# A two-layer trunk on one core: four modulation units of the second layer moved from the first layer's attention to the second's

## The reference

```python
def _modulation(cond, w, b):                       # w: 1024 x 6144, per layer
    m = jax.nn.silu(cond) @ w + b
    return tuple(t[:, None, :] for t in jnp.split(m, 6, axis=-1))

for l in range(2):
    sh, sc, g, shf, scf, gf = _modulation(cond, w_mod[l], b_mod[l])     # once for each group
    h = _adaln(x, norm_mix[l], sh, sc)             # rmsnorm(x) * (1 + sc) + sh
    x = x + g * (attention(h @ w_in[l]) @ w_out[l])    # l = 0: GQA and differential, l = 1: windowed
    n = _adaln(x, norm_ffn[l], shf, scf)
    scores = softmax(n @ w_router)                 # 16 experts, best group of 4, top 2 in it
    x = x + gf * sum_e gate_e * ((silu(n @ w_gate[l, e]) * (n @ w_up[l, e])) @ w_down[l, e])
```

## Time and profile before

| | |
|---|---|
| three runs | 1251.59, 1253.26, 1253.58 us; median 1253.26 |
| the profiled execution | 1251.47 us, of which 1249.7 us from the first to the last instruction |
| PE matmuls | busy 1170.3 us, 94% |
| DVE, ACT, POOL | 280.0, 187.2 and 56.4 us |
| DMA | 494.13 MB, mean 395 GB/s; the SP's queue fills 93.9% of 16 engines' time |
| chain that ended last | PE 73%, DMA 20%, issue 4% |
| first layer | attention to 195 us, experts to 634 us |
| second layer | attention to 806 us, experts to 1243 us, outputs to the end |

### The profile page before, as it was taken

One profiled execution on the slowest core, in us unless ns is written; L12 is line 12 of the kernel. 1 busy time (PEld: TensorE's weight loads), 2 busy tenths in 40 slices (PEclk: granted clock), 3 DMA queues, 4 the chain that ended last, 5 costly groups with the idle time before them and its releaser, 6 DMA issues.

```text
span 1249.7 us, 13688 instructions
## 1 busy us (share of the span) xinstructions
PE 1170.3 (94%) x5491; PEld 511.9 (41%) x5491; DVE 280.0 (22%) x677; ACT 187.2 (15%) x439; POOL 56.4 (5%) x68
## 2 busy tenths in 40 slices
PE   4999999999988998998999999999999899889998
PEld 2445454443423343333344454653434334343433
DVE  1146533121010102020233253312021110102013
ACT  1224322010000000000122342210001101000010
POOL 0412000000000000000013020000000000000000
PEclk9999999999999999999999999999999999999999
DMA  9999999999999999999994578899999999999997
GB/s 375 388 365 382 417 417 430 422 431 427 425 427 428 428 428 428 428 429 428 419 386 150 214 287 329 333 405 425 422 387 428 428 427 428 428 430 428 428 423 306
DMA packets 62820, 494.13 MB, mean 395 GB/s; under 512 B 5795, under 2 KB 6963, under 8 KB 31285
## 3 DMA queue, kind: packets, MB, share of 16 engines
q1 hardware_dynamic: 59728, 485.85, 93.9%
q0 software_dynamic: 2864, 7.46, 1.9%
q10 hardware_dynamic: 180, 0.17, 0.0%
HBM read 490.69 MB, written 3.16 MB: 395 GB/s over the span
## 4 chain that ended last, share of the span: by engine, by line
PE 73%; DMA 20%; issue 4%; ACT 1%; DVE 1%; SPq 1%; POOL 0%; DVEq 0%; POOLq 0%
PE bank L1131 40%; PE bank L902 12%; DMA ring<-in_w_gate 10%; DMA ring<-in_w_up 7%; PE bank L912 3%; PE bank L1090 3%; PE bank L1099 3%; PE bank L858 3%; PE bank L1157 2%; DMA ring<-in_w_in_ab 2%; PE bank L834 2%; DMA ring<-in_w_down 1%; PE bank L1187 1%; PE bank L950 1%; PE bank L1170 1%
## 5 line engine op out<-in xcount | busy, mean ns | idle before, releaser
L1131 PE MATMUL bank<-ring,hT 128*64 128x512 f32 x2592 | 595.0, 609 | 53.2 <-issue 23.4
L1131 PEld LDWEIGHTS bank<-ring,hT 128*64 128x64 f32 x2592 | 199.0, 140 | 417.2 <-issue 415.7
L902 PE MATMUL bank<-ring,hT 128*128 128x512 f32 x320 | 141.9, 601 | 3.1 <-DMA ring<-in_w_in_ab 2.4
L902 PEld LDWEIGHTS bank<-ring,hT 128*128 128x128 f32 x320 | 60.4, 192 | 80.0 <-issue 77.4
L1905 DVE TENSOR_TENSOR work<-work,bank 128x512 f32<-128x512 f32 x56 | 38.5, 688 | 188.8 <-PE bank L1099 188.6
L1898 DVE TENSOR_TENSOR work<-work,bank 128x512 f32<-128x512 f32 x32 | 22.0, 687 | 229.6 <-PE bank L1131 198.6
L1090 PE MATMUL bank<-work 128*128 128x128 f32 x512 | 61.5, 279 | 0.0
L1090 PEld LDWEIGHTS bank<-work 128*128 128x128 f32 x512 | 59.9, 195 | 1.7 <-issue 1.6
L1448 ACT ACTIVATE hT<-bank 128x512 f32<-128x512 f32 x32 | 19.0, 595 | 255.7 <-PE bank L1187 255.7
L912 PE MATMUL bank<-ring,work 128*128 128x512 f32 x128 | 56.5, 594 | 0.3 <-DVE work L1722 0.3
L1946 DVE COPY work<-bank 128x512 f32<-128x512 f32 x14 | 9.7, 692 | 206.3 <-PE bank L1131 206.3
(11 more groups left out here) (214 smaller groups left out, 729.6 us busy)
## 6 DMA issues: line engine op xcount, KB each, us to landing
ring<-in_w_gate SPq DMA_DIRECT2D x58, 2048.0 KB, 17.1
ring<-in_w_up SPq DMA_DIRECT2D x50, 2048.0 KB, 17.2
ring<-in_w_down SPq DMA_DIRECT2D x50, 2048.0 KB, 16.9
ring<-in_w_mod SPq DMA_DIRECT2D x23, 2048.0 KB, 11.3
work<-in_w_up SPq DMA_DIRECT2D x8, 2048.0 KB, 15.5
ring<-in_w_down SPq DMA_DIRECT2D x16, 1024.0 KB, 13.7
ring<-in_w_in_c SPq DMA_DIRECT2D x6, 2048.0 KB, 20.6
ring<-in_w_in_ab SPq DMA_DIRECT2D x4, 2048.0 KB, 21.6
```

The lines of the kernel that those rows point to most:

```text
L902: ins = pe.matmul(b[:, 0:n], hT[:, c, t * P:(t + 1) * P], w[:, c, 0:n], start=i == 0, stop=i == DC - 1)
L1131: ins = pe.matmul(bank[banks[j]][64 * e:64 * e + 64, :], lhs[:, 4 * h + c, 64 * e:64 * e + 64], weights(e, c, j), start=(h, c) == (0, 0), ...
```

## The change

Four things change together.

1. The four units `("mod", 1, 1, k)` leave the first layer's list and the end of `dense_units(0)`. They are loaded behind the input projection of the second layer, and PE uses them at the points "scores" (two), 0 and 1 of the second layer's attention. The group's transposes stand at point 2, and group 2 follows one turn later, with two of its units at point 3.
2. The first expert units of the first layer go straight into the freed slots (`free` is 4 in place of 0; 3 in place of 2 in the second layer), and both layers load the first waiting units in halves.
3. The shift's logits of the second layer are computed in its routing, as in the first layer; and the token rows' logits there stand ahead of the second output projection. Their place in `last_scatter` is taken by `keep_busy(8)`.
4. The first projection of a layer waits for all modulated rows again; `keep_busy(7)` stands ahead of it in the second layer, and `keep_busy` of 8 takes the place of the two units that stood in the first layer's routing.

The diff, cut to its core:

```diff
-        (6,): [("mod", 1, 1, 0)],
         6: [("oT", 0)],
-        (7,): [("mod", 1, 1, 1)],
-        7: [("hT", 1, 1), ("wo", 0, 0), ("rt", 1), ("hk", 1), ("wo", 1, 0), ("rc",), ("xT",), ("mod", 1, 1, 2),
-            ("rt", 0), ("hT", 1, 0), ("mod", 1, 1, 3), ("hk", 0), ("pos",), ("nextT", 1)]},
+        7: [("hT", 1, 1), ("wo", 0, 0), ("rt", 1), ("wo", 1, 0), ("rc",), ("xT",),
+            ("rt", 0), ("hT", 1, 0), ("hk", 0), ("pos",)]},
...
-        "scores": [("in", 2, 0), ("in", 3, 0)],
-        0: [("in", 4, 0)],
-        1: [("T", 0), ("mod", 1, 2, 0), ("in", 5, 0)],
-        2: [("mod", 1, 2, 1)],
-        3: [("mod", 1, 2, 2)],
+        "scores": [("in", 2, 0), ("mod", 1, 1, 0), ("in", 3, 0), ("mod", 1, 1, 1)],
+        0: [("in", 4, 0), ("mod", 1, 1, 2)],
+        1: [("T", 0), ("mod", 1, 1, 3), ("in", 5, 0)],
+        2: [("modT", 1), ("mod", 1, 2, 0)],
+        3: [("mod", 1, 2, 1), ("mod", 1, 2, 2)],
...
-        7: [("hT", 1, 1), ("wo", 0, 0), ("hk", 1), ("wo", 1, 0), ("rt", 1), ("xT",),
+        7: [("hT", 1, 1), ("wo", 0, 0), ("rt", 1), ("wo", 1, 0), ("rc",), ("xT",),
             ("rt", 0), ("hT", 1, 0), ("hk", 0), ("pos",)]}}
...
     if kind == "rt":
-        return [("rt", l, rest[0])]
+        return [("rt", l, rest[0])] + (banks_of(l, ("hk", 1)) if rest[0] else [])
...
-        return mods(0, 0) + inputs + mods(0, 1) + mods(0, 2) + mods(1, 0) + out + mods(1, 1)
+        return mods(0, 0) + inputs + mods(0, 1) + mods(0, 2) + mods(1, 0) + out
     scales = mods(1, 2)
-    return inputs + scales[0:2] + out + scales[2:4]
+    return inputs + mods(1, 1) + scales[0:2] + out + scales[2:4]
...
-                free = 2 * l
+                free = (4, 3)[l]
...
-                if l == 1:
-                    load_halves(0, MOE_UNITS - 2, 1)
-                    load_halves(1, 0, 2)
-                else:
-                    for k in range(SLOTS + AHEAD, MOE_UNITS):
-                        load_early(0, k)
+                load_halves(0, MOE_UNITS - 2, 1)
+                load_halves(1, 0, 2)
...
-                first = (u, t) == (0, 1)
                 for h in range(2):
-                    if not first:
-                        pe.wait_ge(*emptied_by(("hT", l, 0, t, h)))
-                for i in range(DC):
-                    c = 4 * ((i + 1) % 2) + i // 2
-                    if first and i < 6:
-                        pe.wait_ge(chunk_ready[("dve", "act")[i % 2]], 3 * l + i // 2 + 1)
+                    pe.wait_ge(*emptied_by(("hT", l, 0, t, h)))
...
-                if l == 1:
-                    pe.wait_ge(mod_emptied, 6)
-                    keep_busy(2)
+                pe.wait_ge(mod_emptied, 4 + 2 * l)
+                keep_busy(2 if l else 8)
...
                         if (l, t) == (0, 1):
-                            shift_logits(1)
+                            keep_busy(8)
...
-                keep_busy(3 if l else 2)
+                keep_busy(3)
...
                 if l == 1:
                     norm(1, 0, 1)
+                    keep_busy(7)
```

More of the change, by code:

```diff
@@ L434, in build @@
         one, other = ("modT", 0, 0), ("hT", 0, 0, 1, 1)
-        done_at[one], done_at[other] = done_at[other], done_at[one]
-        one, other = ("rt", 1, 1), ("xT", 1, 0)
         done_at[one], done_at[other] = done_at[other], done_at[one]
@@ L656, in experts @@
                 load_kept(1, 2)
-                sp.wait_ge(gates_taken, 3 + l)
-                sp.wait_ge(filled, fill(("modT", 1, 1 + l)))
+                sp.wait_ge(gates_taken, 2 * l + 2)
+                sp.wait_ge(filled, fill(("modT", 1, 2 * l)))
                 load_kept(1, 3, 1)
-                if l == 1:
-                    load_halves(0, MOE_UNITS - 2, 1)
-                    load_halves(1, 0, 2)
-                else:
-                    for k in range(SLOTS + AHEAD, MOE_UNITS):
-                        load_early(0, k)
+                load_halves(0, MOE_UNITS - 2, 1)
+                load_halves(1, 0, 2)
                 for n in (1, 2):
-                    for k in range(2 * l if n == 1 else 0, MOE_UNITS):
+                    for k in range(2 if n == 1 else 0, MOE_UNITS):
                         if (n, k) == (1, SLOTS):
@@ L842, in mod @@
                     pe.wait_ge(mod_emptied, 3 * l + group)
-                if (l, group, k) == (1, 2, 0):
-                    pe.wait_ge(shift_taken, 1)
                 for r in range(2):
@@ L875, in norm @@
                     transposes(("hT", l, kind, t, h), [channels(xn(kind, t), 4 * h + i) for i in range(4)])
-                if (l, kind, t) == (1, 1, 0):
-                    keep_busy(5)
+                if (kind, t) == (1, 0):
+                    keep_busy(5 if l else 8)
             def keep_busy(times, where=sums_bank):
@@ L891, in project @@
                 b = bank_free(("qkv", l, u, t))
-                first = (u, t) == (0, 1)
                 for h in range(2):
-                    if not first:
-                        pe.wait_ge(*emptied_by(("hT", l, 0, t, h)))
-                for i in range(DC):
-                    c = 4 * ((i + 1) % 2) + i // 2
-                    if first and i < 6:
-                        pe.wait_ge(chunk_ready[("dve", "act")[i % 2]], 3 * l + i // 2 + 1)
-                    elif first:
-                        pe.wait_ge(*emptied_by(("hT", l, 0, t, (i + 1) % 2)))
-                    ins = pe.matmul(b[:, 0:n], hT[:, c, t * P:(t + 1) * P], w[:, c, 0:n], start=i == 0, stop=i == DC - 1)
+                    pe.wait_ge(*emptied_by(("hT", l, 0, t, h)))
+                for c in range(DC):
+                    ins = pe.matmul(b[:, 0:n], hT[:, c, t * P:(t + 1) * P], w[:, c, 0:n], start=c == 0, stop=c == DC - 1)
                 ins.then_inc(filled, 1)
@@ L1122, in product @@
                     pe.wait_ge(ready, 2 * n + 1 + h)
-                    by_halves = early and l == 1 and (n, k) in ((0, 0), (0, 2))
-                    if early and l == 1 and (n, k) in ((0, MOE_UNITS - 2), (1, 0)):
+                    by_halves = early and (n, k) in ((0, 0), (0, 2))
+                    if early and (n, k) in ((0, MOE_UNITS - 2), (1, 0)):
                         pe.wait_ge(m["half_loaded%d" % n], 32)
@@ L1188, in hidden_transposed @@
                     ins.then_inc(m["ht_done"], 1)
-                last = number["modT", 1, 1] if l == 0 else number["count", 1]
+                last = number["count", l]
                 before, behind = ([jobs[k][0] for k in range(last - 6, last + 1) if (bank_of(jobs[k][0]) is bank[1]) == first] for first in (True, False))
@@ L1309, in modulate @@
                 for c in range(8 if (kind, t) == (1, 0) else 4):
-                    if (kind, t) == (0, 1) and c:
-                        ins.then_inc(chunk_ready["act"], 1)
                     if c == 4:
@@ L1591, in prompt_rows @@
             def prompt_rows(l):
-                if l == 0:
-                    name = ("rc", 0)
-                    dve.wait_ge(filled, fill(name))
-                    dve.tensor_copy(rc[:, :], bank_of(name)[:, 0:NE]).then_inc(emptied["dve"], 1)
+                name = ("rc", l)
+                dve.wait_ge(filled, fill(name))
+                dve.tensor_copy(rc[:, :], bank_of(name)[:, 0:NE]).then_inc(emptied["dve"], 1)
                 name = ("xT", l, 1)
```

33 lines of the change are left out of this document (9 added, 24 removed).

## The result

| | median us | all executions | ratio to before (95%) |
|---|---|---|---|
| before | 1252.42 | 1250.56 to 1253.58 (4) | |
| changed, first time | 1266.39 | 1259.48, 1265.16, 1267.63, 1268.40 | 1.0110 (1.0092 to 1.0128) |
| changed, second time | 1264.66 | 1261.84 to 1269.67 (6) | 1.0107 (1.0087 to 1.0126) |

The change makes the kernel 12 to 14 us slower by the medians (13.4 to 13.8 by the ratios); 8 had been forecast. The first measurement lies above the range of 1256.0 to 1265.0, the second just inside it. The changed kernel's executions spread from 1259.48 to 1269.67, over 10 us; those of before spread over 3 in the first measurement and over 6 in the second (1250.03 to 1255.94). The profiled execution of the first time is the shortest, 1259.48 us (span 1257.7, 8.0 over before's), so its trace shows the forecast rather than the surplus. A second trace is needed for that.

The account below looks back on a forecast made before the run. PE was taken to bound the first experts and the second layer's attention, with no free slots for transfers running further ahead. Terms summed to +7.8 us: 1259.3 from the profiled execution, 1261.0 from the median; range 1256.0 to 1265.0.

Parts of the forecast that it names:

- transfers of the first layer: First layer's experts: four units (8.39 MB) fewer to load, mostly becoming idle time; -1.0 us, bounds 0 to -2.2.
- start of its experts: First layer, ahead of its experts: values of turns 6 and 7 start earlier without two units; -1.6 us.
- start of the second layer: Second layer's first projection waits for the whole modulation, not two chunks; +0.9 us, bounds 0.6 to 1.4.
- units in the second layer: Second layer's attention: four units at 1.85 us of PE each plus the group's transposes at 0.7; +8.1 us.
- routing: Second layer's routing: one more set of logits in PE's row, +1.7 us, less 0.3 for DVE's earlier steps.
- gates: Second layer's attention gates, now computed there and sent through HBM: no cost in the sum, slack growing to 5.5 us.
- a lead of the transfers finds no free slot: First layer's experts: transfers running further ahead find memory full; of any lead, 2.1 us can be used.
- rival of the bytes: First layer's experts hang on the byte stream alone and end 19.6 us earlier; 1244 us, 6%.
- hidden units: Second layer's attention: PE only fills a chain through ACT and DVE, so units cost half; 1257 us, 12%.
- The four loads fall where 267 of 427 GB/s move: 0: Second layer's attention: the moved units' four loads fit into free bandwidth and land before use; 0 us.
- First expert loads begin two turns later in the program order, and have the same 50 us to the first product: 0: Second layer: first expert loads, later in program order, still have 50 us before their first product; 0 us.
- the gates come late: Second layer's attention: gates' read slowed by expert loads beside it, PE stalls 3 to 5 us; 1264 to 1266, 12%.

Follow-up runs that it names:

- a_outs_behind: Changed kernel, with POOL's second-layer outputs of keys and values issued behind the gates' write and read; 1258.32 us, ratio 1.0056 to before.
- b_outs: Kernel before, with only POOL's second-layer outputs of keys and values moved behind the gates; ratio 1.0005 to before.
- b_free3_outs: Kernel before, with a third early expert load in the second layer and POOL's outputs of keys and values behind the gates; ratio 1.0002.
- b_free3: Kernel before, with a third second-layer expert load ahead of the last scores, nothing else; 1253.52 us, ratio 1.0022, executions up to 1261.23.
- b_hf22: Kernel before, with two first-layer expert loads ahead of the last scores and first waiting units loaded in halves in both layers; ratio 1.0038.
- b_halves_only: Kernel before, with the halves in the first layer too and no other load moved; ratio 1.0000 over 12 executions.
- b_parts34: Kernel before, with parts 3 and 4 of the change alone, units and loads as before; ratio 1.0020.
- a_loads_wait: Changed kernel, with SP's first expert loads of the second layer held until the gates have landed; 1258.39 us, ratio 1.0056.

## Why the prediction was wrong

With the gates' way cleared the changed kernel is 6.1 us over before by its medians (1258.3 against 1252.25; 7.0 by the ratio). The terms of the sum, each as forecast and as the traces have it:

| term | forecast | measured | from |
|---|---|---|---|
| transfers of the first layer | -1.0 | -2.1 | experts 439.3 and 437.2 |
| start of its experts | -1.6 | -2.2 (or -0.6) | 194.97 and 192.73 (or 194.4) |
| start of the second layer | +0.9 | +0.9 | 7.1 and 8.0 from product to projection |
| units in the second layer | +8.1 | +7.8 | 172.41 and 164.57 |
| routing | +1.4 | +1.5 | 164.57 and 163.11 |
| sum | +7.8 | +5.9 | |
| gates | 0 | +6 to +8 | with and without either cure |

172.41 is the stretch in a_outs_behind, 163.11 that in b_outs, which runs the routing of before:

```profile
639.55 7.11 PE L886 MATMUL bank<-ring,hT 128*128 128x512 f32 x16
...
811.96 7.09 PE L1115 MATMUL bank<-ring,hT 128*64 128x512 f32 x32 [0.78 <-ACT hT L1426]
```

```profile
642.20 7.11 PE L905 MATMUL bank<-ring,hT 128*128 128x512 f32 x16 [0.67 <-DVE hT L1589]
...
805.31 7.09 PE L1134 MATMUL bank<-ring,hT 128*64 128x512 f32 x32 [0.78 <-ACT hT L1446]
```

Before's own 164.3 had the half clock of the earlier trace rows in it, worth 1.2 us: b_free3_outs has it too (164.3), while b_outs, b_free3, b_hf22 and b_halves_only take 163.1. Three things in the table are less firm than its numbers look.

- The first product of the first layer stands at 192.7 to 192.9 in five of nine traces of the changed kernel and its variants, at 194.4 in three, a_outs_behind among them, and at 196.9 in one, though what they do up to there differs in the early loads at most. In a_outs_behind the granted clock is 0.70 over 190 to 195 us; in the changed kernel's first trace it is 1.00. So of the -2.2 some executions keep only 0.6, and the sum is then 7.5. The spans fit: the five traces of the changed kernel in which PE doesn't wait for the gates and nothing is left out are 5.1 to 6.6 us over before's.
- The -2.1 is between two traces. Of the kernel before and its variants without halves, five traces have 438.4 to 439.3 us; of the changed kernel and its variants, seven have 437.0 to 437.2 and two 438.0 and 438.4.
- The +1.5 of the routing does not show once the second layer's experts are added to the stretch: 601.6 us in b_parts34, 601.2 to 601.9 in six traces with the routing of before. Where the half clock lies in the stretch (before, b_free3_outs) the experts take 437.0 and 437.1 us; in the other four they take 438.2 to 438.8.

**Right:** the direction, that PE and not bytes bounds the second layer's attention, the price of a unit, the start of the second layer, the size of the routing in its stretch, and that a lead of the transfers finds no free slot. With the gates' way cleared the whole sum, +7.8, comes out at 6.1 to 7.0. The rival of the bytes (1244) and that of the hidden units (1257) are both out: the experts of the first layer shrank by 2 us and not by 19.6, and the units cost 7.8.

**Mis-sized:** the first layer's two terms, both inside their bounds. For the transfers about the whole 2.1 us of queue were gained, where I took the middle.

**Wrong:** the step that costs what goes with the units at nothing. "The four loads fall where 267 of 427 GB/s move: 0" and "First expert loads begin two turns later in the program order, and have the same 50 us to the first product: 0" asked whether those loads come in time for their own users. They do: even 15 us later they cost nothing (a_loads_wait). What they do is sit beside another transfer which has a user 5 us away. The third early load of part 2 is counted nowhere in the sum. With the gates at nothing the forecast lost 6 to 8 us.

The rival "the gates come late" named the mechanism, the place (the transposes of turn 6) and its time, 1264 to 1266; measured were 1266.4 and 1264.7. Its sum can be checked against the traces, in us from the second layer's first projection:

| | before | forecast | changed, first | changed, second |
|---|---|---|---|---|
| read issued | 116.8 | +5.6 | +5.5 | +8.1 |
| gates landed | 120.9 | +5.6 | +12.6 | +14.4 |
| slack of PE | 3.0 | 5.5 | none, waits 1.68 | none, waits 3.52 |

So in the first trace the write came out as reckoned and the read alone took 7 us more; in the second the write took 2.5 us more as well. Taken from the forecast slack of 5.5 us, the 7.0 and 8.8 us give waits of 1.5 and 3.3, as traced. The rival had 12% for two reasons. I took the write's duration as given, though its 14 us for 8 KB said that it stood behind something. And I let the slack grow on a read of 4.2 us, though I had noted that no row showed that read beside other transfers: it was the read in an idle queue. The timeline of SP's queue in the kernel before shows that nothing was issued between 745.4 and 760, and over 755 to 758 us the data moved had fallen to 16 GB/s:

```profile
740.33 5.08 SPq L558 DMA_DIRECT2D ring<-in_w_gate  x2
759.99 0.33 SPq L558 DMA_DIRECT2D work<-in_w_up  x1
```

Here the trace agrees with the rule of the Trainium skill, "DMA: Bandwidth & Descriptors", section "Issuing engines are not separate DMA queues", that transfers of different engines interleave: 4.2 us alone, 10.5 to 12 beside ring loads. The rule should have moved the chance.

One reading behind the rival of the bytes was loose: DMA is not full from the start. The first four slices of the earlier trace rows move 365 to 388 GB/s, not 428. Nothing in the sum rests on it.

**Open:** the stall as traced costs 2.8, 4.8 and 7.1 us (stretches of 175.2, 177.2 and 179.5 against 172.4), the last with 0.8 us of its own order in it. Executions of 1268 to 1270 were not traced; whether they hold a longer wait or more half clock is not settled. The mean granted clock of the three over 1267.5 us is 0.980, against 0.986 in the shortest, but a low mean alone doesn't make the time: an execution of before with 0.979 took 1252.83. That the 8 MB give the first layer's 2.1 us is by exclusion. Where b_hf22 loses its 5 us is not known.

## What to carry to other kernels

A stage with free bandwidth may still hold one small transfer on the critical path. Before filling such a stage, list the small transfers in it, their slack to the user, and what lies ahead of them in their own queue and beside them in others; price them in a full queue, not as they stand. A spread of the times that grows with a change is a hint of such a race, and one profiled execution can be the lucky one. The cure here was to issue the small, urgent transfer ahead of the large ones whose users come later.

## What the hardware showed unexpectedly

- A write of 8 KB in two transfers held POOL 12 to 16 us behind 1 MB of outputs on the same queue, 8.65 us behind them with SP's expert loads held back, and 5 to 6 us ahead of them. A read of 512 KB took 4.2 us in an idle queue and 10.5 to 12 us beside loads of SP.
- A wait of PE cost more than itself: 2.8 us for one of 1.68, 4.8 for one of 3.52. About 1 us of that is lost with the granted clock at 1.00, by waits for ACT and DVE. Behind the waits of 3.52 and 4.71 us the granted clock fell (0.72 over 777 to 783 us in both), and a unit took 2.82 and 3.59 us in place of 1.92; that added only 0.1 to 0.5 us to the way to the next output projection. Behind the wait of 1.68 us it did not fall, in one trace.
- A lone matmul in one quarter of the array's columns took 1.04 us for its two records, as long as four in the four quarters (1.07 us for eight).
